# Scattering the experts' rows: plain fp32 products of one y against fp32r products of its hi and lo parts

## The reference

```
gates = top-2 softmax weights of each token inside its best group of 4 (16 experts, 4 groups)
out = 0
for e in range(16):
    a = silu(h @ w_gate[e]) * (h @ w_up[e])        # h: 256 x 1024, FF = 512
    out = out + gates[:, e] * (a @ w_down[e])      # w_down[e]: 512 x 1024
x = x + out
```

## Time and profile before

| | us |
|---|---|
| median of 3 executions | 725.13 |
| lowest, highest | 722.84, 726.81 |
| profiled execution | 724.94 |
| its span from first to last instruction | 722.0 |
| TensorE / VectorE / ScalarE busy | 657.2 / 510.4 / 426.3 |

### The profile page before, as it was taken

One profiled execution on the slowest core, in us unless ns is written; L12 is line 12 of the kernel. 1 busy time (PEld: TensorE's weight loads), 2 busy tenths in 40 slices (PEclk: granted clock), 3 DMA queues, 4 the chain that ended last, 5 costly groups with the idle time before them and its releaser, 6 DMA issues.

```text
span 722.0 us, 8750 instructions
## 1 busy us (share of the span) xinstructions
PE 657.2 (91%) x3028; PEld 522.4 (72%) x3028; DVE 510.4 (71%) x578; ACT 426.3 (59%) x472; POOL 24.2 (3%) x14
## 2 busy tenths in 40 slices
PE   6999999999989999999788499989998999799984
PEld 5887888778767788888667477667766777577763
DVE  4544868635844388676544669986999699969993
ACT  6526547447544373445537087758776777778760
POOL 0100000301000000000002100000000000000000
PEclk9999999999999999999988599989998999989998
DMA  9963647635433365550680068996799789978921
GB/s 342 323 231 120 229 168 274 209 129 162 142 88 111 126 218 179 182 175 1 227 348 39 0 233 303 392 387 253 295 382 389 264 293 377 394 268 310 361 103 58
DMA packets 61052, 164.02 MB, mean 227 GB/s; under 512 B 4345, under 2 KB 9147, under 8 KB 52828
## 3 DMA queue, kind: packets, MB, share of 16 engines
q1 hardware_dynamic: 56432, 158.81, 60.4%
q10 hardware_dynamic: 4588, 4.80, 2.0%
HBM read 162.53 MB, written 2.64 MB: 229 GB/s over the span
## 4 chain that ended last, share of the span: by engine, by line
PE 57%; DVE 24%; issue 9%; ACT 5%; DVEq 4%; DMA 1%; POOL 0%; ACTq 0%; SPq 0%
DVE w_lo L1224 14%; PE ps L1438 13%; PE ps L1446 13%; PE ps L1439 13%; PE ps L1787 5%; PE ps L1419 3%; DVEq L1365 3%; PE ps L1769 2%; DVE y_lo L1347 2%; PE ps L1581 1%; PE ps L1606 1%; PE ps L1817 1%; ACT w_hi L758 1%; DVE e_act L1366 1%; DVE e_act L1369 1%
## 5 line engine op out<-in xcount | busy, mean ns | idle before, releaser
L897 DVE TENSOR_TENSOR w_lo<-w_raw,w_hi 128x2048 fp32r<-128x2048 f32 (+2 forms) x54 | 118.5, 2211 | 53.9 <-ACT w_hi L498 53.3
L1438 PE MATMUL ps<-w_hi,act_hi 128*128 128x512 f32 (+1 forms) x304 | 118.0, 390 | 1.1 <-ACT w_hi L498 1.1
L498 ACT ACTIVATE w_hi<-w_raw 128x2048 fp32r<-128x2048 f32 (+2 forms) x54 | 99.1, 1855 | 29.5 <-PE ps L1446 28.7
L1439 PE MATMUL ps<-w_hi,act_lo 128*128 128x512 f32 (+1 forms) x304 | 116.2, 384 | 0.0
L1224 DVE TENSOR_TENSOR w_lo<-w_raw,w_hi 128x2048 fp32r<-128x2048 f32 (+1 forms) x48 | 99.8, 2110 | 11.1 <-ACT w_hi L758 11.0
L1224 DVE TENSOR_TENSOR w_lo<-e_raw,w_hi 128x2048 fp32r<-128x2048 f32 (+2 forms) x48 | 97.1, 2064 | 7.5 <-ACT w_hi L758 7.5
L758 ACT ACTIVATE w_hi<-w_raw 128x2048 fp32r<-128x2048 f32 (+1 forms) x48 | 84.8, 1770 | 1.3 <-PE ps L1790 1.0
L758 ACT ACTIVATE w_hi<-e_raw 128x2048 fp32r<-128x2048 f32 (+2 forms) x48 | 82.6, 1729 | 2.1 <-PE ps L1787 1.5
L1787 PE MATMUL ps<-w_hi,xg 128*128 128x512 f32 x236 | 75.1, 436 | 0.0
L1446 PE MATMUL ps<-w_lo,act_hi 128*128 128x512 f32 (+1 forms) x304 | 74.1, 386 | 0.0
L1438 PEld LDWEIGHTS ps<-w_hi,act_hi 128*128 128x128 f32 x304 | 57.1, 188 | 14.6 <-issue 1.6
(11 more groups left out here) (311 smaller groups left out, 980.3 us busy)
## 6 DMA issues: line engine op xcount, KB each, us to landing
w_raw<-in_w_in SPq DMA_DIRECT2D x32, 1024.0 KB, 5.4
w_raw<-in_w_expert_gate SPq DMA_DIRECT2D x24, 1024.0 KB, 7.0
e_raw<-in_w_expert_down SPq DMA_DIRECT2D x24, 1024.0 KB, 8.9
w_raw<-in_w_expert_up SPq DMA_DIRECT2D x16, 1024.0 KB, 6.6
e_raw<-in_w_expert_up SPq DMA_DIRECT2D x16, 1024.0 KB, 7.2
e_raw<-in_w_expert_gate SPq DMA_DIRECT2D x8, 1024.0 KB, 9.2
w_raw<-in_w_expert_down SPq DMA_DIRECT2D x8, 1024.0 KB, 7.6
w_raw<-in_w_xkv SPq DMA_DIRECT2D x4, 1024.0 KB, 5.7
```

What stands on the lines that cost most here:

```text
L498: A(bview(w_hi, b, blocks[b].shape), bview(w_raw, b, blocks[b].shape), ACT.Copy).then_inc(hi_done, 1)
L897: V.tensor_tensor(bview(w_lo, b, sh), bview(w_raw, b, sh), f32(bview(w_hi, b, sh)), ALU.subtract).then_inc(lo_done, 1)
L1438: MM(o, xh[:, t0 + k, i * P:(i + 1) * P], wh[:, k], start=first and k == 0, stop=False)
L1439: MM(o, xl[:, t0 + k, i * P:(i + 1) * P], wh[:, k], start=False, stop=False)
```

## The change

The scaled result of an expert is kept once, as float32 (`y_rows`), and `selT` is float32 as well. The scatter makes one plain fp32 product where it made two fp32r products: four for each expert in place of eight. `y_lo_part` on VectorE is removed, and all waits for `y_lo_done` become waits for `y_done`, which ScalarE raises with its copy. On ScalarE the copy stays, with another output type.

```diff
-        selT = sb("selT", [P, EPG, S], f32r)
+        selT = sb("selT", [P, EPG, S])
-        y_hi, y_lo = sb("y_hi", [P, D], f32r), sb("y_lo", [P, D], f32r)
+        y_rows = sb("y_rows", [P, D])
...
-            def y_hi_part(q, m, j):
+            def y_out(q, m, j):
                 act.wait_ge(mm_done, GB * q + (NB1 + 2 * m + 2))
                 act.wait_ge(s["scattered"], FREE + EPG * q + j)
                 for half in range(2):
-                    ins = A(y_hi[:, half * COLS:(half + 1) * COLS], ps[:, 2 + half, :], ACT.Copy, scale=w_slot[:, j:j + 1])
-                ins.then_inc(s["y_hi_done"], 1)
+                    ins = A(y_rows[:, half * COLS:(half + 1) * COLS], ps[:, 2 + half, :], ACT.Copy, scale=w_slot[:, j:j + 1])
+                ins.then_inc(s["y_done"], 1)
...
-            def y_lo_part(q, j):
-                dve.wait_ge(s["y_hi_done"], FREE + EPG * q + (j + 1))
-                for half in range(2):
-                    cs = slice(half * COLS, (half + 1) * COLS)
-                    ins = V.scalar_tensor_tensor(y_lo[:, cs], ps[:, 2 + half, :], w_slot[:, j:j + 1], f32(y_hi[:, cs]),
-                                                 ALU.mult, ALU.subtract)
-                ins.then_inc(s["y_lo_done"], 1)
...
-                    elif which == "down":
-                        y_lo_part(q, j)
-                        if more and j == 1:
-                            select(q + 1, g + 1)
+                    elif which == "down" and more and j == 1:
+                        select(q + 1, g + 1)
...
-                y_lo_part(q, EPG - 1)
...
             def turn_selection(q):
-                pe.wait_ge(s["y_lo_done"], FREE + EPG * q)
+                pe.wait_ge(s["y_done"], FREE + EPG * q)
...
             def e_turn(q, j):
-                pe.wait_ge(s["y_lo_done"], FREE + EPG * q + j)
+                pe.wait_ge(s["y_done"], FREE + EPG * q + j)
...
             def e_scatter(q, j):
-                pe.wait_ge(s["y_lo_done"], FREE + EPG * q + (j + 1))
+                pe.wait_ge(s["y_done"], FREE + EPG * q + (j + 1))
                 for i in range(NT):
                     for half in range(2):
-                        for y in (y_hi, y_lo):
-                            ins = MM(ps[:, 4 + 2 * i + half, :], selT[:, j, i * P:(i + 1) * P],
-                                     y[:, half * COLS:(half + 1) * COLS], start=False, stop=False, skip_group_check=True)
+                        ins = MM(ps[:, 4 + 2 * i + half, :], selT[:, j, i * P:(i + 1) * P],
+                                 y_rows[:, half * COLS:(half + 1) * COLS], start=False, stop=False, skip_group_check=True)
                 ins.then_inc(s["scattered"], 1)
```

More of the change, by code:

```diff
@@ L276, in build_program @@
             sel_ready sel_turned selT_moved gathered gathered_moved slot_gates_done gu_moved
-            gu_turned gate_summed gate_tanh_done a_ready y_hi_done y_lo_done scattered moe_done ws_masked
+            gu_turned gate_summed gate_tanh_done a_ready y_done scattered moe_done ws_masked
             out_ready half_rsqrt_ready slot_gates_moved xq_ready zeros_written""".split()
@@ L836, in expert_group @@
                     else:
-                        y_hi_part(q, m, j)
+                        y_out(q, m, j)
                 if more:
@@ L843, in expert_group @@
                     gathered(q + 1, range(2, 4))
-                y_hi_part(q, len(ex_order) - 1, EPG - 1)
+                y_out(q, len(ex_order) - 1, EPG - 1)
                 if more:
@@ L850, in expert_group @@
                     e_hi(q, n)
-            for name in ("y_hi_done", "gu_moved"):
+            for name in ("y_done", "gu_moved"):
                 act.drain().then_inc(s[name], FREE)
@@ L1341, in slot_gates @@
                 V.tensor_tensor(w_slot_next[:], w_slot_next[:], diagonal(EPG), ALU.add).then_inc(s["slot_gates_moved"], 1)
-            def y_lo_part(q, j):
-                dve.wait_ge(s["y_hi_done"], FREE + EPG * q + (j + 1))
-                for half in range(2):
-                    cs = slice(half * COLS, (half + 1) * COLS)
-                    ins = V.scalar_tensor_tensor(y_lo[:, cs], ps[:, 2 + half, :], w_slot[:, j:j + 1], f32(y_hi[:, cs]),
-                                                 ALU.mult, ALU.subtract)
-                ins.then_inc(s["y_lo_done"], 1)
             def expert_group(q, g, more):
                 dve.drain()
-                dve.wait_ge(s["y_hi_done"], FREE + EPG * q)
+                dve.wait_ge(s["y_done"], FREE + EPG * q)
                 V.tensor_copy(w_slot[:], w_slot_next[:])
@@ L1388, in _ @@
             select(0, 0)
-            dve.drain().then_inc(s["y_lo_done"], FREE)
             with dve.Fori(0, rounds) as r:
```

## The result

The changed kernel takes 737.05 us (median of four, 736.7 to 737.4), the kernel before 725.15 us (722.84 to 726.81, four runs). The ratio is 1.0166, 95% interval 1.0138 to 1.0195: slower, by 12 us. The forecast was 728.6 us, its range 723 to 737.

The account below looks back on a forecast made before the run. TensorE and VectorE were taken as close to a tie: +25.1 us on TensorE, -21.5 of stalls and half clock. Three groups +0.9, last group +2.75: 724.94 + 3.65 = 728.6 us, range 723 to 737.

Parts of the forecast that it names:

- TensorE's cost: Each scatter: four fp32 products of 0.86 us, 3.43 us instead of 1.86; +1.57 us for each of 16, 25.1 in all.
- The middle stretches: Second and third stretch of a group: TensorE sets the pace, 17.2 us (+1.1) and 16.8 us (+0.1).
- Idle time at a change: Group change, before the second gather tile: VectorE's reduce starts earlier, chain -1.45 us, TensorE's idle time from 3.2 to 1.8.
- The failed step: Group changes: after only 1.8 us of idle time the clock stays full, saving 2.6 us at each of three.
- forecast of -2.5: From third scatter to fourth at a group change: -2.5 us each, three times.
- The end: Last group from its third scatter on: +0.2 us, clock falling as before; 1.6 us less if it holds.
- The part ahead of the experts: Work until the first scatter: no change, 0 us.
- The first rival: Group changes: the clock falls all the same, because the whole thin time matters; 3 x 2.6 = 7.8 us, 736.4 us, chance 0.20.
- the second and third: Rivals: VectorE alone bounds the kernel, 702 us, chance 0.08; w_lo stays late in middle stretches, 735 us, chance 0.07.
- The loads' share: Second stretch: weight loads 11.44 of 16.09 us, 71%, suggesting 29% of TensorE free; called a view that could mislead.

Follow-up runs that it names:

- Relief alone: Changed kernel with the scatter back at eight fp32r products, y's one part used twice, y_lo gone: 711.36 us against 725.92 for the kernel before, ratio 0.9789.
- turn first in it: Kernel before with the transposes of gate and up rows moved ahead of the scatter: 725.49 us, ratio 0.9999.
- one part: Changed kernel with y and the selection as fp32r, four products, lo part of y left out: 706.86 us, ratio 0.9760.
- cost alone: Kernel before with the scatter as four plain fp32 products, y_lo still written by VectorE but not multiplied: 734.92 us, ratio 1.0108.
- five with idle time filled or covered: Zero products: changed kernel 728.29 us, kernel before 718.6, one part 701.75, kernel before with two more fp32 tiles 716.21; changed kernel, transposes before scatter: 727.81.
- the cut scatter: Changed kernel with each scatter cut in two, token tile 0 before the transposes and tile 1 after: 722.87 us, ratio 0.9941.

## Why the prediction missed

- TensorE's cost, 0.86 us for a plain fp32 product and 3.43 for a scatter: right (3.43).
- The middle stretches, a near tie that TensorE takes over: right to 0.05 us. Relief alone gave 15.59 and 15.20 for 15.6 and 15.2. VectorE is not busy for 2.2 and 1.9 us of them now (17.17 - 14.95, 16.77 - 14.89).
- Idle time at a change from 3.2 to 1.8 us, by a chain that starts 0.65 us after the transposes: right (0.67 and 1.78).
- **The failed step: "idle time shorter than 3.2 us can pass at full clock. I take it that 1.8 us does: -2.6."** It rested on a single idle stretch of 2.80 us in one profile, at another place: before the last scatter. At that very place the clock held in five of six profiles that have the 2.80 us. At the group changes it did not: with 1.7 to 1.9 us of idle time the clock fell at 9 of 12, for 3.4 us each, three times of three in the changed kernel's first profile and twice in its second. In the first the three stretches ended 1.4, 1.4 and 1.7 us above their forecast of -2.5, some 4.5 us in all.
- The end: half clock was taken as before. It lasted 6.8 us instead of 3.4, 1.6 us more.
- The part ahead of the experts was taken as unchanged; it is 2.55 us longer in these two profiles, and 2.37 of them are there by the 82nd matmul record, at about 26 us. That record starts at 25.50 and 26.40 us in the two profiles of the kernel before, at 25.83 to 28.61 in the four kernels built from it, and at 25.52 to 27.98 in the eight profiles of the changed kernel and of those built from it. So this start varies within either family of kernels. Another difference between profiles is a fall of the clock at about 217 us, behind 2.1 us of idle time that all fourteen have: it comes in eight of them, and not in the first two. TensorE's instructions up to there are the same in all, so that the difference comes of the change is not shown. But the first scatter starts at 440.7 and 441.6 us in the kernel before and at 443.1 to 447.5 in all twelve others, those built from the kernel before included, and why it was early twice stays open.

So the experts' part grew by 9.2 us instead of 3.65: 4.5 and 1.6 for the clock, and 0.5 less than forecast in the stretches that were right. The other 2.55 us lie ahead of it. The first rival (half clock at the changes in spite of the shorter idle time) named what happened, with a price that was too high: 7.8 us, for half clock of 6.8 us at each change, where 3.4 us of it cost some 4.5 in all. Its total of 736.4 us lies near the measured 737.05 by luck, since 1.6 us at the end and 2.55 ahead of the experts, which it did not have, make up for that; the second and third are refuted by 128 records and by stretches without a wait. The fall had been given a chance of 0.20.

Idle time of TensorE and half clock behind it, over all fourteen profiles. The first three rows are the idle time before the second gather tile at a group change:

| idle time shown | kernels | with half clock | its length |
|---|---|---|---|
| 2.7 to 3.2 us | before (twice), turn first in it, one part | 12 of 12 | 6.8 us |
| 1.7 to 1.9 us | after (twice), relief alone, cost alone | 9 of 12 | 3.4 us |
| 0.9 us or less | five with idle time filled or covered, and the cut scatter | 0 of 18 | |
| 2.8 us before the last scatter | those that wait there for y_lo | 1 of 6 | 6.8 us |
| 2.8 to 3.5 us before the last down projection | after (twice), relief alone, cost alone, turn first in before | 3 of 5 | 3.4 or 6.8 us |
| 4.3 to 4.4 us at the same place | before (twice), one part | 3 of 3 | 3.4 us |
| 2.1 us at about 217 us | all | 8 of 14 | 6.8 or 10.2 us |

This table is what one profile could not give. At the group changes longer idle time goes with more half clock. Across places the length alone does not order it: 2.8 us before the last scatter, with 512-column products ahead of it, fell once in six, and 1.7 to 1.9 us behind transposes and eight-column products 9 times in 12. That is the side of the first rival, but no run changed what stands ahead of the idle time and left its length as it was, so the cause of the fall stays open. The loads' share that the prediction set aside stayed a bad guide: the Trainium skill (Perfetto Trace Analysis, Identifying the Most-Contended Engine) judges TensorE's headroom by it, beside the share of peak arithmetic, and as to the loads' share this trace disagrees. In the second stretch after the change it is 11.53 of 17.17 us, 67%, less than before, on a TensorE without any gap.

## What to carry to other kernels

Where two engines are within a few per cent of each other, price a trade of work by the one that will be late after it, from distances between starts: here 1.32 us off VectorE for 1.57 us on TensorE lost. The relief was worth 14.6 us only as long as TensorE's work did not grow. Idle time on TensorE costs its own length and then, where the clock falls, 1.3 to 1.5 us more for 3.4 us of half clock and up to 2.9 us (6.64 against 3.70 for the last scatter) for 6.8; put work that is ready into it, but look what that work was covering where it stood. One execution does not tell whether the clock will fall: give such a step its chance, and price both ways.

## What had not been expected of the hardware

- The clock's fall behind the same idle time differs from change to change within one execution (16.01 and 17.55 us for the same instructions), and from execution to execution.
- Less work can cost time: one part of y in place of a doubled one lengthened the group change from 16.09 to 17.33 us, with 2.9 us of idle time instead of 1.9 and half clock for 6.8 us instead of 3.4.
- Products with a tile of zeros, which add nothing to the result, in the idle time keep the clock at 1.00: with two of them at each group change and three at the end, the changed kernel's experts' part is 7.0 us shorter.
